# A hybrid encoder's mixing stage: SyncE issues the rotary half swaps and the weight loads in the order of one plan, and the shared rotary key is projected onto 128 partitions at once

## The reference

```python
z = rmsnorm(h, nm) @ w_in[l]                   # 1024 -> 1824 columns
u, va, q, k, vb, cq, ckv_raw, kpe_raw = split_proj(z)   # 256,256,512,128,128,384,128,32
# A: chunk MLP
a = u * (w_s @ va + b)                         # per 128 positions, 4 groups, masked
# B: sliding window attention, 8 query heads on 2 key heads of 64, with sinks
q, k = rope(q), rope(k)
b = softmax([q k^T / 8, sink]) @ vb
# C: latent attention, 4 heads
qc = rmsnorm(cq, g_q) @ w_uq                   # 384 -> 4 x (64 + 32)
q_nope, q_pe = qc[..., :64], rope(qc[..., 64:])
ckv = rmsnorm(ckv_raw, g_kv)
kpe = rope(kpe_raw)                            # 32 columns, shared by the 4 heads
s = ((q_nope w_uk^T) ckv^T + q_pe kpe^T) * 96 ** -0.5
c = (softmax(s) @ ckv) w_uv
h = h + concat(a, b, c) @ w_out[l]
```

## Time and profile before

| what | value |
|---|---|
| time, median of 3 runs | 2058.07 us (2057.37 to 2061.0) |
| time of the profiled execution | 2061.27 us |
| its span | 2059.5 us |
| PE busy | 2031.5 us, 99% of the span |
| VectorE, ScalarE, GpSimd busy | 82%, 47%, 17% |
| mixing, layer 0 and layer 1 | 220 and 218 us |

### The profile page before, as it was taken

How to read it: one execution, slowest core, us unless ns; L and a number is a source line. 1 busy time by engine, 2 the same in 40 slices (tenths; PEclk the granted TensorE clock), 3 DMA queues, 4 the chain that set the end, 5 groups by cost and what they waited for, 6 DMA issues and landing times. The chain is left out here.

```text
span 2059.5 us, 41110 instructions
## 1 busy us (share of the span) xinstructions
PE 2031.5 (99%) x15435; PEld 1975.0 (96%) x15435; DVE 1683.0 (82%) x2481; ACT 978.1 (47%) x1776; POOL 359.7 (17%) x219
## 2 busy tenths in 40 slices
PE   8999999999999999999989999999999999999998
PEld 7999999999889999999989999999997899999998
DVE  5999998756666999998899999976657589999975
ACT  6544453324545544463465655533345474444532
POOL 0322200033011222200022222001321112222000
PEclk8999999999999999999999999999999999999999
DMA  4232332352112222322223222324321122232331
GB/s 133 83 102 84 99 92 79 92 129 65 45 54 83 83 88 96 97 88 86 78 83 102 88 95 79 112 79 118 95 68 32 55 82 91 94 102 79 94 96 65
DMA packets 236727, 178.35 MB, mean 87 GB/s; under 512 B 35808, under 2 KB 231616, under 8 KB 236608
## 3 DMA queue, kind: packets, MB, share of 16 engines
q1 hardware_dynamic: 231712, 170.36, 27.8%
q10 hardware_dynamic: 4896, 6.36, 1.1%
HBM read 170.12 MB, written 3.62 MB: 84 GB/s over the span
## 5 line engine op out<-in xcount | busy, mean ns | idle before, releaser
L1471 PE MATMUL pair<-t_parts,chunk_high 128*128 128x288 f32 x4592 | 916.7, 295 | 6.3 <-POOL chunk_low L827 2.6
L1471 PEld LDWEIGHTS pair<-t_parts,chunk_high 128*128 128x128 f32 x4592 | 736.8, 188 | 8.0 <-POOL chunk_low L827 3.2
L1471 PE MATMUL pair<-t_parts,chunk_low 128*128 128x288 f32 x2296 | 677.7, 295 | 0.0
L1471 PEld LDWEIGHTS pair<-t_parts,chunk_low 128*128 128x128 f32 x2296 | 431.4, 188 | 0.0
L827 POOL TENSOR_TENSOR chunk_low<-set_raw,chunk_high 128x512 fp32r<-128x512 f32 x164 | 236.6, 1453 | 872.1 <-ACT chunk_high L926 872.1
L926 ACT ACTIVATE chunk_high<-chunk_sum 128x512 fp32r<-128x512 f32 x328 | 203.8, 630 | 372.5 <-DVE chunk_sum L2024 190.4
L821 POOL TENSOR_TENSOR w_low<-raw,w_high 128x1024 fp32r<-128x1024 f32 (+2 forms) x48 | 115.7, 2414 | 620.7 <-ACT w_high L874 620.7
L2036 DVE TENSOR_TENSOR chunk_low<-chunk_sum,chunk_high 128x512 fp32r<-128x512 f32 x328 | 214.5, 695 | 9.2 <-ACT chunk_high L926 1.9
L1418 PE MATMUL pair<-hidden_high,w_high 128*128 128x288 f32 x896 | 191.9, 296 | 0.0
L1418 PE MATMUL pair<-hidden_high,w_low 128*128 128x288 f32 x896 | 191.9, 296 | 0.0
L1418 PE MATMUL pair<-hidden_low,w_high 128*128 128x288 f32 x896 | 191.8, 296 | 0.0
(11 more groups left out here) (304 smaller groups left out, 3727.0 us busy)
## 6 DMA issues: line engine op xcount, KB each, us to landing
set_raw<-in_w_up_dram SPq DMA_DIRECT2D x44, 1024.0 KB, 5.3
...
raw<-in_w_in_dram SPq DMA_DIRECT2D x16, 256.0 KB, 3.9
...
raw<-in_w_out_dram SPq DMA_DIRECT2D x16, 256.0 KB, 4.1
```

The costliest lines, as they stand in the source:

```text
L1471: mm = nc.tensor.matmul(out, c[:, j, p, :], tr[p // 2][:, seat(p), x, t, :], start=p == 0 and n == 0, stop=p == KP - 1 and n == 2)
```

## The change

`PLAN` is a new list. It has new entries, `d:`NAME, at which SyncE issues the load of a slot (`d:st` the stores, `d:in2` the late tables), and SyncE now walks through the list too (`feed_mixing`). The `sw:` entries belong to SyncE instead of ScalarE: at each it waits until the source is emptied and issues the four transfers. The slot kpe now holds only the 32 columns of each k, and ScalarE and GpSimd read them four times over (`four_times`, `by_head`), so that its high and low parts are 1024 columns wide with the key's columns repeated for the four heads; `z:kpe` becomes a plain product with x whose 128 rows are the repeated key, and is emptied straight into `kpe_rep`. `rep`, `rep32` and its load at the start are gone. The rotary columns of w_uq have a buffer of their own, loaded with the late tables from SyncE's queue, and a new step `uq` makes their high part on ScalarE and their low part on VectorE. The order of PE's steps and their pairs are changed throughout.

```diff
-        return {"q": 2, "kpe": 1 + KQ, "qn": KQ}.get(WIN[s - ZIN][:1] if WIN[s - ZIN][0] == "q" and WIN[s - ZIN] != "qn" else WIN[s - ZIN], 1)
+        return {"q": 2, "qn": KQ}.get(WIN[s - ZIN][:1] if WIN[s - ZIN][0] == "q" and WIN[s - ZIN] != "qn" else WIN[s - ZIN], 1)
     return 1
...
-        return {"kpe": KD * C_ROPE + KQ * P, "qn": 2 * KQ * P}.get(WIN[s - ZIN], SLOT)
+        return {"qn": 2 * KQ * P}.get(WIN[s - ZIN], SLOT)
...
-PLAN = """z:k@0 w:q0 sumx@1 w:q1 sw:k z:v@2 w:q2 rot:k z:q0@0 tw@2 z:q1@1 w:q3 sw:q1 rot:q1 w:va0 tc@2 w:va1 sw:q0
-ex:0 rot:q0 z:q2@0 z:q3@2 sw:q2 tv@0 rot:q2 w:u0 sw:q3 S:0@1 E:0 z:va0@3 rot:q3 z:va1@0 w:u1 T:0@3 tva:0@1 S:1@2 S:2@3
-E:1 tva:1@1 w:ckv z:u0@0 w:cq0 T:1@1 E:2 z:u1@2 w:cq1 O:0@3 O:1@1 w:cq2 a:0@0 a:1@3 T:2@1 z:ckv@0 w:kpe S:3@3 S:4@1
-E:3 z:cq0@0 T:3@3 sumkv@2 w:qn E:4 z:cq1@0 O:2@1 w:A0 S:5@2 z:cq2@0 T:4@1 E:5 z:kpe@3 O:3@2 O:4@1 S:6@3 T:5@2 qn:0@1
-E:6 sumq@2 S:7@0 rep@3 T:6@1 w:A1 tckv@2 qp@3 A:3@1 E:7 rkv@3 O:6@2 O:5@1 S:8@3 rot:qp@0 T:7@2 E:8 vc:0@1 kn:1@2 A:1@0
-S:9@1 T:8@2 rot:kpe@0 E:9 kn:0@3 vc:1@2 O:8@1 O:7@3 T:9@2 MS:0@0 ME:0 qn:1@3 A:4@2 w:B0 MT:0@0 tk@1 MS:1@3 O:9@0
-MO:0@1 ME:1 w:B1 MS:2@2 tkpe@1 A:5@3 MT:1@1 MS:3@0 ME:2 A:7@1 A:0@2 A:2@3 MT:2@1 B:0@2 ME:3 MO:2@1 w:B2 MO:1@0 MS:4@2
-MT:3@3 ME:4 B:2@0 MS:5@2 MT:4@3 ME:5 A:6@0 MS:6@3 MO:3@2 MT:5@1 MS:7@0 ME:6 MO:5@2 w:B3 MO:4@1 B:1@3 MT:6@1 ME:7 B:3@2
-MS:8@0 ex:1 MT:7@1 ME:8 B:5@3 MO:6@0 MO:7@1 MS:9@3 MT:8@0 ME:9 B:4@2 MT:9@3 w:C0 B:6@0 MO:8@2 MO:9@3 B:7@1 w:C1""".split()
+PLAN = """d:q2 w:q0 z:k@0 sumx@1 w:q1 d:q3 d:va0 z:v@2 w:q2 sw:k rot:k z:q0@0 w:q3 z:q1@2 w:va0 d:va1 ex:0 sw:q1 d:u0
+w:va1 sw:q0 rot:q0 z:q2@0 d:u1 rot:q1 w:u0 sw:q2 z:q3@2 tv@0 S:0@1 E:0 rot:q2 d:ckv d:cq0 sw:q3 w:u1 tk@3 rot:q3
+z:va0@2 w:ckv tc@3 tw@1 w:cq0 z:va1@0 T:0@2 tva:0@1 S:1@3 d:cq1 d:cq2 S:2@0 d:kpe d:qn d:A0 tva:1@2 E:1 z:u0@1 T:1@3
+w:cq1 E:2 z:u1@2 O:0@0 a:1@3 a:0@2 O:1@0 T:2@3 w:cq2 z:ckv@1 S:3@3 S:4@0 O:2@1 E:3 z:cq0@2 T:3@1 w:kpe E:4 sumkv@3
+z:cq1@2 S:5@3 S:6@0 T:4@2 w:qn E:5 z:cq2@1 O:3@2 z:kpe@3 d:in2 w:A0 T:5@2 qn:1@1 E:6 d:A1 sumq@2 w:A1 qn:0@3 tckv@0
+O:4@2 O:5@1 S:7@3 d:B0 T:6@0 uq A:2@1 A:1@2 E:7 qp@0 A:7@2 rkv@3 S:8@1 T:7@0 rot:qp@2 E:8 vc:0@3 O:6@0 O:7@2 S:9@1
+T:8@3 rot:kpe@0 E:9 kn:0@2 A:6@3 w:B0 kn:1@1 d:B1 MS:0@2 d:B2 tkpe@3 d:B3 T:9@1 MS:1@0 d:st ME:0 O:8@3 O:9@1 MS:2@2
+MT:0@1 ME:1 w:B1 A:3@3 vc:1@1 A:0@0 MT:1@1 ME:2 B:1@3 ex:1 MO:1@2 MO:0@1 MS:3@0 MS:4@1 MT:2@2 ME:3 B:3@3 w:B2 A:5@2
+MT:3@0 ME:4 A:4@3 w:B3 MO:3@0 MO:2@2 MS:5@1 MT:4@3 ME:5 MS:6@0 B:5@3 MT:5@1 ME:6 B:0@2 MO:4@0 d:C0 MO:5@1 MS:7@3
+MT:6@1 MS:8@0 ME:7 B:2@2 MT:7@3 ME:8 B:4@1 MO:7@0 MO:6@3 MS:9@1 MT:8@0 ME:9 w:C0 B:7@2 MT:9@1 MO:8@0 d:C1 w:C1 MO:9@1
+B:6@2""".split()
...
-SLOT_STEPS[ZIN + WIN.index("kpe")].append("qp")
...
-        "rot": lambda: [] if arg == "kpe" else ["qp.0"],
-        "rep": lambda: ["z:kpe.0"],
+        "rot": lambda: ["z:kpe.0"] if arg == "kpe" else ["qp.0"],
...
-        "qp": lambda: ["z:cq2.1"],
+        "qp": lambda: ["z:cq2.1", "uq.0"],
...
+        def four_times(s):
+
+            return raw[s % RAW][:, 0:KD * C_ROPE].rearrange("p (k c) -> p k c", c=C_ROPE).unsqueeze(2).broadcast_to([P, KD, C_HEADS, C_ROPE])
+
+        def by_head(t):
+            return t[:, :].rearrange("p (k h c) -> p k h c", h=C_HEADS, c=C_ROPE)
 
...
-        N_MIX_IN = MIX_IN_FIRST + 16 * 3
+        N_MIX_IN = MIX_IN_FIRST + 16 * (3 + KQ)
...
-            def w_in(layer):
+            def w_in(layer, zs_):
...
-                    if n == 3:
-                        mix_loads(layer)
...
+            def late_tables(layer):
+
+                pe_did(sp, layer, "z:kpe")
+                stand_alone(sp)
+                sp.dma_start(cos32[:, :], a["rope"][2]).then_inc(mix_in, 16)
+                sp.dma_start(sin32[:, :], a["rope"][3]).then_inc(mix_in, 16)
+                sp.dma_start(rot32[:, :], a["const"][2]).then_inc(mix_in, 16)
+                uq = a["mla_w_uq"][layer].rearrange("(k p) (h n) -> p k h n", p=P, n=C_NOPE + C_ROPE)
+                for k in range(KQ):
+                    sp.dma_start(uq_raw[:, k, :].rearrange("p (h n) -> p h n", h=C_HEADS), uq[:, k, :, C_NOPE:]).then_inc(mix_in, 16)
+
+            def half_swap(layer, z):
+
+                dve_did(sp, layer, f"z:{z}.0")
+                stand_alone(sp)
+                b = SWAPPED.index(z) % 2
+                for r in range(0, P, 32):
+                    sp.dma_start(zr[b][r:r + 32, :], zs[b][r ^ 32:(r ^ 32) + 32, :]).then_inc(swap_in[b], 16)
+
+            def feed_mixing(layer):
+
+                w_in(layer, WIN[:RING])
+                mix_loads(layer)
+                for step in MIX:
+                    kind, _, name = step.partition(":")
+                    if kind == "sw":
+                        half_swap(layer, name)
+                    elif step == "d:st":
+                        stores(layer)
+                    elif step == "d:in2":
+                        late_tables(layer)
+                    elif kind == "d" and name in WIN:
+                        w_in(layer, [name])
+                    elif kind == "d":
+                        w_out(layer, name[0], int(name[1]))
 
             for layer in range(DEPTH):
                 gate_up(layer, 0, a["w1_up"], a["w1_gate"])
                 down(layer, F1D, a["w1_down"], 2 * layer)
-                w_in(layer)
-                w_out(layer)
+                feed_mixing(layer)
...
+                if s == ZIN + WIN.index("kpe"):
+                    nc.gpsimd.tensor_tensor(out=by_head(wl[s % RING]), in0=four_times(s), in1=by_head(wh[s % RING]).bitcast(F32),
+                                            op=ALU.subtract).then_inc(low_ready, 1)
+                    return
...
+                if s == ZIN + WIN.index("kpe"):
+                    nc.scalar.activation(by_head(wh[s % RING]), four_times(s), ACT.Copy).then_inc(high_ready, 1)
+                    return
...
-                    if kind == "sw":
-
-                        dve_did(act, layer, f"z:{arg}.0")
-                        b = SWAPPED.index(arg) % 2
-                        for r in range(0, P, 32):
-                            act.dma_start(zr[b][r:r + 32, :], zs[b][r ^ 32:(r ^ 32) + 32, :]).then_inc(swap_in[b], 16)
-                        continue
                     if not scalar_ops(step):
-                        if step == "z:kpe":
-
-                            did("z:kpe")
-                            act.dma_start(cos32[:, :], a["rope"][2]).then_inc(mix_in, 16)
-                            act.dma_start(sin32[:, :], a["rope"][3]).then_inc(mix_in, 16)
-                            act.dma_start(rot32[:, :], a["const"][2]).then_inc(mix_in, 16)
                         continue
                     if kind == "z":
 
...
+                    if kind == "uq":
+                        act.wait_ge(mix_in, layer * N_MIX_IN + N_MIX_IN)
+                        copy(uq_high[:, :, :], uq_raw[:, :, :], "uq.0")
                         continue
...
-                    elif kind == "rep":
-                        copy(two(kpe_rep[:, :]), halves(p), "rep.0")
...
-                            def tile_kpe(t, k):
-                                return t[s % RING][:, k * C_ROPE:k * C_ROPE + P]
-                            mm = product(p, [(tile_kpe(wh, k), tile_kpe(wl, k), xh[:, k, :], xl[:, k, :]) for k in range(KD)])
...
-                    elif kind == "rep":
-
-                        for half in range(2):
-                            mm = nc.tensor.matmul(ps[p][:, half, 0:HALF], rep32[:, :], zs[0][0:C_ROPE, half * HALF:(half + 1) * HALF], start=True, stop=True)
...
-                        off = KD * C_ROPE
-                        mm = product(p, [(*tile_w(s, k, off), cqh[:, k, :], cql[:, k, :]) for k in range(KQ)])
+                        mm = product(p, [(uq_high[:, k, :], uq_low[:, k, :], cqh[:, k, :], cql[:, k, :]) for k in range(KQ)])
...
-                            adid("rep.0")
+                            own("z:kpe.0")
...
+                    elif kind == "uq":
+                        adid("uq.0")
+                        emit(nc.vector.tensor_tensor(uq_low[:, :, :], uq_raw[:, :, :], uq_high[:, :, :].bitcast(F32), ALU.subtract), names[0])
```

More of the change, by code:

```diff
@@ L213, in scalar_ops @@
     n = {"z": 0, "sumx": 1, "sumkv": 2, "sumq": 4, "tw": 1, "tv": 2, "tc": 2, "tk": 2, "tva": 2,
-         "rkv": 2, "tkpe": 2, "rep": 1, "a": 1, "kn": 1, "E": 5, "O": 1, "ME": 2, "MO": 1, "ex": 1}.get(kind, 0)
+         "rkv": 2, "tkpe": 2, "uq": 1, "a": 1, "kn": 1, "E": 5, "O": 1, "ME": 2, "MO": 1, "ex": 1}.get(kind, 0)
     if kind == "vc":
@@ L230, in vector_ops @@
     kind, arg = split(step)
-    n = {"z": 1, "sumx": 2, "sumq": 3, "tckv": 2, "tw": 1, "rot": 3, "a": 4, "qp": 1, "qn": 1,
+    n = {"z": 1, "sumx": 2, "sumq": 3, "tckv": 2, "tw": 1, "rot": 3, "a": 4, "qp": 1, "qn": 1, "uq": 1,
          "O": 1, "MO": 1, "A": 1, "B": 1, "E": 4, "ME": 2}.get(kind, 0)
@@ L253 @@
 assert [s[2:] for s in MIX if s[:2] == "w:"] == MSLOTS[2:]
```

(24 more changed lines are left out.)

32 lines of the change are left out of this document (16 added, 16 removed).

## The result

| kernel | median | lowest to highest | runs |
|---|---|---|---|
| before | 2057.49 us | 2056.74 to 2061.0 | 11 |
| changed | 2062.91 us | 2061.39 to 2066.03 | 11 |

The ratio is 1.0027, with a 95% interval of 1.0019 to 1.0035: 5.4 us more, where 4.1 us less was forecast, and outside the forecast's range. The profiled execution of the changed kernel took 2062.81 us for a span of 2061.0.

The account below looks back on a forecast made before the run. TensorE, busy 99% of the span, was taken as the bound. Terms -2.3 - 4.9 - 1.2 - 0.8 - 0.8 + 4.0 + 0.9 + 1.0 gave -4.1 us from the median 2058.07: 2054.0, range 2048.5 to 2059.0 (forecast's own 2051.5 to 2056.5).

Parts of the forecast that it names:

- + 4.0 (new waits for swaps): Mixing stages: swaps issued late from SyncE's queue make PE wait 2.0 us per layer, 4.0 in all.
- 0.4 us at z:q2: PE waits 0.4 us (0 to 1.8) for the pair that z:q0 leaves late, behind k's swap.
- 1.4 at S:0: PE waits 1.4 us (0 to 3) at the first scores, for VectorE's rotation of q1.
- tv does not wait: At step tv, PE was to find its pair emptied in time, so no wait was counted.
- 4.9 (early waits): PE's waits in mixing before S:1 and tv, and others early in the stages, would go: -4.9 us.
- 1.2 and 0.8 for the two dips: PE's two drops to 1.2 GHz in mixing: -1.2 us for layer 0's, -0.8 for half of layer 1's.
- rep, -2.3: Removing rep's four matmuls ahead of T:6 saves PE 1.16 us per layer, 2.3 us for two.
- MO:9, +1.0: MO:9, now close behind MT:9, waits for ScalarE's copy of it: 0.5 us per layer, +1.0 (0.4 to 2.4).
- the 0.9 for some seven steps: Steps T:2, T:9, MT:2, MT:3, MO:3, MT:4, MT:7, with thin cover: 0.9 us for all, both layers (0 to 4).
- C: Rival, slower: k's late swap sets the stage's pace, z:q2 waits 4.2 us per layer, clock drops; 2064, chance 0.10.
- B: Rival, gain given back: slow swaps, S:0 waits 2.0 us and S:1 again 1.1 us; 2057.4, chance 0.24.
- A: Rival: the order covers everything, no new wait for swaps, both dips gone; 2047.7, chance 0.16.

Follow-up runs that it names:

- the second profile: The changed kernel run again without any further edit, for a second profile and more times: 2063.59 us, ratio 1.0026 to before.
- The second profile of before: The kernel before, run again unchanged for another profile: median 2058.95 us; its profiled execution took 2058.06 us, span 2056.3.
- the reversed edit: Four matmuls of rep's size put back ahead of T:6 in the changed kernel with its swaps ahead of the loads: 2053.97 us, against 2051.24.

## Why the prediction was wrong

**The step that failed first: the price of the swaps in SyncE's queue.** "+ 4.0 (new waits for swaps)", made of 0.4 us at z:q2, 1.4 at S:0 and "tv does not wait", with 0 and 9 as ends, measured 9.1 us (8.7 in the second profile): z:q2 1.5, tv 0.8 to 1.0, S:0 1.5, T:0 0.5 to 0.8. The mechanism was laid out rightly, with d:va0 ahead of sw:k, u0's load ahead of q0's swap and both meetings with a low part; its size was taken too low. At z:q2, PE and SyncE were both earlier than laid out, by 0.9 and 1.0 us. k's swaps then took 5.1 us from the first issue to the last landing, 429.79 to 434.88, where 4.4 was put down (the last of the four 3.2, where 2.5 was), and from there to z:q0's leaving its pair 4.5 us, where 4.1 was: 1.1 us more of wait in all. q0's swaps began 0.8 us later than laid out and took 5.0 us (443.76 to 448.75), where 4.7 was, and with the meeting behind them z:q2 was out at 453.4 instead of 452.0: so tv waited after all. S:0's 1.5 us is what was forecast, but came on top of the wait at tv. T:0's wait stood nowhere in the sum.

The page "DMA: Bandwidth & Descriptors" of the Trainium skill, on queues, rings and completion order, was read in the prediction as speaking against the change, since each queue's ring is consumed in order. These runs do not bear that reading out: the delay behind a load went with how closely the swap followed it, and was there from the other queue too. The whole 4.2 us of a load, drawn from the page as a limit, is shown nowhere; what a load just ahead costs is 3.5 us instead of 2.0. What held k's swap was, with 5.2 us, SyncE's waiting to be allowed the load ahead of it; a cost of the ring itself is not shown.

**The second: what before had to give.** "4.9 (early waits)", and 1.2 and 0.8 for the two dips of the earlier trace rows, were taken from one execution that took 3.2 us more than the median, and were subtracted from the median; "nothing in the sum depends on that offset" was wrong. The second profile of before has 4.4 us of these early waits and no dip. So this was worth about 0.5 + 2.0 = 2.5 us.'s two dips cost that execution 3.4.

**The third: no price for PE's clock behind the new waits.** The forecast had the clock at 1.00; the changed kernel fell to 1.2 GHz behind tv and S:0 once in one profile and in both layers in the other, 1.7 us each time.

**Right:** rep, -2.3, as the reversed edit shows in this order (2.7 measured); S:1's wait gone, q3's swap under its cover; T:3's gone; q1 served in time; nearly no cost of the wide slot or of uq. In the old order the key's part of the change costs 12.7 us. **Too high:** MO:9, +1.0, where PE stood about 0.1 us per layer, and the 0.9 for some seven steps, none of which waited: 0.2 us at another step is all. Together, 5.1 us for the swaps, 2.5 for before and 1.7 or 3.4 for the clock, less 1.5 for the terms put too high, are 7.8 to 9.5 us, of the 9.5 between the forecast's -4.1 and the measured +5.4.

**Summed again** from the second profile of before (2056.3): -2.3 for rep, +4.0 for the waits (9.3, with that 0.2, against 5.3) and +1.7 for one dip are +3.4 us, where the span grew by 4.7; in the second profile of the changed kernel, -2.3 + 3.7 + 3.4 = +4.8, where it grew by 5.7. In these 1.3 and 0.9 us stay without a name.

**The rivals.** None names the outcome. C had the mechanism, sw:k held behind a load, and nearly the time, 2064, but put it in one 4.2 us wait at z:q2. B expected S:1 to wait again; it did not. A, 2047.7, lies 3 us below what the same order reaches once three entries of its list are moved, 2051.
